# Feed-forward down products: token sums by halves, a second group one piece later, and last blocks between last products

## What is computed

```python
def swiglu(x, w_gate, w_up, w_down):
    return (jax.nn.silu(x @ w_gate) * (x @ w_up)) @ w_down

x = x + 0.5 * swiglu(rmsnorm(x, ffn1_norm[l]), ffn1_w_gate[l], ffn1_w_up[l], ffn1_w_down[l])
```

## Time and profile before

| what | value |
|---|---|
| median of three runs | 1376.59 us |
| the profiled execution | 1378.8 us |
| its span, first to last instruction | 1377.0 us |
| TensorE (PE) busy | 1331.3 us, 97% |
| VectorE (DVE) busy | 930.1 us, 68% |
| ScalarE (ACT) busy | 817.0 us, 59% |
| GpSimd (POOL) busy | 476.5 us, 35% |
| mean granted TensorE clock | 0.987 |

### The profile page before, as it was taken

One profiled execution on the slowest core, in us unless ns is written; L12 is line 12 of the kernel. 1 busy time (PEld: TensorE's weight loads), 2 busy tenths in 40 slices (PEclk: granted clock), 3 DMA queues, 4 the chain that ended last, 5 costly groups with the idle time before them and its releaser, 6 DMA issues.

```text
span 1377.0 us, 18310 instructions
## 1 busy us (share of the span) xinstructions
PE 1331.3 (97%) x7264; PEld 1119.2 (81%) x7264; DVE 930.1 (68%) x1162; ACT 817.0 (59%) x1095; POOL 476.5 (35%) x220
## 2 busy tenths in 40 slices
PE   9999899999999899999799999999999999999988
PEld 8878777888878788878688887788888888887877
DVE  6678876955669796678785659764335642568887
ACT  7654557457656457655457687667434654665553
POOL 1614013464550504432313431134535524452410
PEclk9999999999999999999999999999999999999999
DMA  9586983324659685668784656345755543648783
GB/s 338 184 235 219 248 269 131 115 93 153 209 148 287 167 266 205 204 159 269 175 282 148 225 180 214 118 158 174 286 182 174 178 168 127 224 154 203 233 221 108
DMA packets 42278, 269.66 MB, mean 196 GB/s; under 512 B 6320, under 2 KB 6864, under 8 KB 11216
## 3 DMA queue, kind: packets, MB, share of 16 engines
q1 hardware_dynamic: 35680, 226.69, 46.8%
q0 software_dynamic: 4608, 33.56, 13.3%
q10 hardware_dynamic: 1904, 8.23, 1.7%
HBM read 267.38 MB, written 1.08 MB: 195 GB/s over the span
## 4 chain that ended last, share of the span: by engine, by line
PE 64%; DVE 16%; POOL 9%; ACT 4%; DMA 3%; issue 2%; SPq 1%; POOLq 0%; ACTq 0%; DVEq 0%
PE acc L392 12%; PE acc L394 11%; PE acc L393 11%; PE acc L407 9%; DVE wlo L373 8%; PE acc L408 5%; POOL forms L1027 4%; POOL forms L1019 4%; DMA raw<-in_t_ffn_down 2%; PE acc L2828 2%; DVE x L936 2%; PE work L661 1%; DVE work L864 1%; DVE form_lo L927 1%; PE work L662 1%
## 5 line engine op out<-in xcount | busy, mean ns | idle before, releaser
L373 DVE TENSOR_TENSOR wlo<-raw,whi 128x2048 fp32r<-128x2048 f32 (+1 forms) x189 | 443.6, 2350 | 125.9 <-ACT whi L368 125.7
L368 ACT ACTIVATE whi<-raw 128x2048 fp32r<-128x2048 f32 (+1 forms) x245 | 460.4, 1886 | 61.1 <-PE acc L394 25.0
L407 PE MATMUL acc<-xT,whi 128*128 128x512 f32 x1208 | 429.8, 398 | 1.4 <-DVE wlo L373 1.3
L373 POOL TENSOR_TENSOR wlo<-raw,whi 128x2048 fp32r<-128x2048 f32 x56 | 270.7, 4835 | 374.7 <-ACT whi L368 366.8
L408 PE MATMUL acc<-xT,wlo 128*128 128x256 f32 x1384 | 373.9, 281 | 0.0
L407 PEld LDWEIGHTS acc<-xT,whi 128*128 128x128 f32 x1208 | 227.0, 188 | 56.2 <-issue 2.5
L408 PEld LDWEIGHTS acc<-xT,wlo 128*128 128x128 f32 x1384 | 261.5, 189 | 7.1
L392 PE MATMUL acc<-whi,xT 128*128 128x512 f32 x416 | 168.4, 405 | 0.0
L394 PE MATMUL acc<-whi,xT 128*128 128x512 f32 x416 | 162.5, 391 | 0.0
L393 PE MATMUL acc<-wlo,xT 128*128 128x512 f32 x416 | 162.3, 390 | 0.0
L774 ACT ACTIVATE hid_hi<-work 128x256 fp32r<-128x256 f32 x88 | 33.7, 383 | 134.1 <-DVE work L873 134.1
(11 more groups left out here) (422 smaller groups left out, 2135.3 us busy)
## 6 DMA issues: line engine op xcount, KB each, us to landing
raw<-in_t_ffn_up SPq DMA_DIRECT2D x85, 1024.0 KB, 5.4
raw<-in_t_m_in SPq DMA_DIRECT2D x52, 1024.0 KB, 5.2
raw<-in_t_ffn_down SPq DMA_DIRECT2D x32, 1024.0 KB, 6.2
raw<-in_t_ffn_down POOLq DMA_DIRECT2D x32, 1024.0 KB, 8.6
raw<-in_t_m_os SPq DMA_DIRECT2D x8, 1024.0 KB, 4.9
raw<-in_t_ffn_down SPq DMA_DIRECT2D x8, 512.0 KB, 4.3
raw<-in_t_m_out SPq DMA_DIRECT2D x4, 1024.0 KB, 5.1
sum_rows<-row_scratch ACTq DMA_DIRECT2D x4, 1024.0 KB, 4.7
```

Of the source, the lines that this page charges most:

```text
L368: act.activation(granule(whi, u, i), granule(raw, u, i), ACT.Copy).then_inc(hi_ready, 1)
L373: eng.tensor_tensor(granule(wlo, u, i), granule(raw, u, i), granule(whi, u, i).bitcast(F32), ALU.subtract).then_inc(lo_signal(g)[0], 1)
L407: pe.matmul(to, hi[:, c], both_parts(kt), start=first, stop=False)
```

## The change

Three things move. GpSimd's two token sums of a group are issued one by one (`sum_hidden(group, j)`), each as soon as its four hidden rows are there, and in other places of its queue. In the order of places the second group starts one piece later. And the last four blocks alternate with the last four products of the second group. Waits, `hi` and `lo` follow the new order; the last two places become places like the others, so that by tokens only the last two rows are multiplied in the last stage.

Places 10 to 39 after: 10 to 24 as before, up18 (25), P4' (26), up19, P6' (28), up20, P3' (30), up21, P7' (32), b0 (16 to 19), P1' (34), b0 (20, 21), P2' (36), b1 (16 to 19) (37), P5' (38), b1 (20, 21) (39). The transposes stand behind place 37.

```diff
 def late_places():
-    for k in range(11):
+    for k in range(len(PRODUCTS)):
         places += [products[k], ("up", 11 + k)]
-    blocks = [("block", half, kts) for half in range(2) for kts in ((16, 17, 18, 19), (20, 21))]
-    return places + [products[11], blocks[0], products[12], blocks[1], products[13], blocks[2], blocks[3]]
+    places.append(("up", 18))
+    for k in range(3):
+        places += [products[7 + k], ("up", 19 + k)]
+    for k, (half, kts) in enumerate(((0, (16, 17, 18, 19)), (0, (20, 21)), (1, (16, 17, 18, 19)), (1, (20, 21)))):
+        places += [products[10 + k], ("block", half, kts)]
+    return places
...
 def multiply_by_token(pe, u, xhi, xlo, banks, last_bank):
-            for i in range(2):
-                if t == 0 and i == 1:
-                    wait_lo(pe, u.g + 1)
-                hi, lo = granule(whi, u, i), granule(wlo, u, i)
-                for j, kt in enumerate(u.granules[i]):
-                    mm = triple(pe, to, xhi, xlo, kt, t, hi[:, j, c], lo[:, j, c], i == 0 and j == 0,
-                                i == 1 and j == len(u.granules[1]) - 1)
+            hi, lo = granule(whi, u, 0), granule(wlo, u, 0)
+            for j, kt in enumerate(u.granules[0]):
+                mm = triple(pe, to, xhi, xlo, kt, t, hi[:, j, c], lo[:, j, c], own and j == 0, j == len(u.granules[0]) - 1)
...
 ffn_tensor:
-                if n == LAST_UNIT - 1 and b + 1 != B_OUT:
-                    transpose_x(pe, b + 1, 0)
...
-                if f == 3 and half == 1:
-                    if n == LAST_UNIT:
-                        multiply_by_token(pe, u, hid_hi, hid_lo, BACK_OF_X, ffn_banks(NCH)[0][:, 0:256])
+                if f == 3 and n == PLACES - 1:
+                    multiply_by_token(pe, u, hid_hi, hid_lo, BACK_OF_X, ffn_banks(NCH)[0][:, 0:256])
                 else:
                     multiply(pe, u, i, hid_hi, hid_lo, ffn_banks(NCH + half), kts[0] == 16, kts[-1] == KFF - 1)
+                if n == 37 and b + 1 != B_OUT:
+                    transpose_x(pe, b + 1, 0)
...
 ffn_scalar:
-            if n == 23:
-                act.wait_ge(gran_done, place_done(f, n))
+            if n == 24:
                 round_forms(1)
-        square_x(act, b + 1, 0)
-        if b + 1 == B_FFN2:
-            square_gained(act, 0)
-        hi(LAST_UNIT + 3)
+            if n == 36:
+                square_x(act, b + 1, 0)
+                if b + 1 == B_FFN2:
+                    square_gained(act, 0)
...
 ffn_vector:
-            if n in (10, 24):
-                rest_forms((10, 24).index(n))
+            if n in (10, 25):
+                rest_forms((10, 25).index(n))
+            if n == 35:
+                for t in range(NT):
+                    dve.wait_ge(*last_added[t, 0])
+                residual_half(dve, b + 1, 0, place_done(f, n), ffn_banks(NCH), HALF_RSTD)
+                if b + 1 == B_FFN2:
+                    apply_final1(dve, 0)
...
             elif entry[0] == "product":
-                if n < 35:
+                if n < 38:
                     lo(n + 3)
-                if n == 35:
-                    lo(38)
-                    lo(39)
                 add_product(n, *entry[1:])
-                if n == 37:
-                    if b == B_FFN0:
-                        dve.wait_ge(params_loaded, 16 * len(PARAMS))
-                    if b + 1 != B_OUT:
-                        rest_xt(dve, b + 1, 0)
-            elif n == 34:
+            elif n < 37:
                 lo(n + 3)
-            elif n == 36:
-                for t in range(NT):
-                    dve.wait_ge(*last_added[t, 0])
-                residual_half(dve, b + 1, 0, place_done(f, n), ffn_banks(NCH), HALF_RSTD)
-                if b + 1 == B_FFN2:
-                    apply_final1(dve, 0)
-                lo(PLACES)
+            elif n == 37:
+                lo(n + 3)
+                if b == B_FFN0:
+                    dve.wait_ge(params_loaded, 16 * len(PARAMS))
+                if b + 1 != B_OUT:
+                    rest_xt(dve, b + 1, 0)
...
 ffn_pool:
-        def make_forms(group):
-            pool.wait_ge(hidlo_done, PIECES * f + KD * (group + 1))
+        def sum_hidden(group, j):
+            pool.wait_ge(hidlo_done, PIECES * f + KD * group + 4 * (j + 1))
             if group:
                 pool.wait_ge(forms_split, 2 * (2 * f + 1))
-            for j in range(2):
-                kts, rows = slice(4 * j, 4 * j + 4), slice(KD * group + 4 * j, KD * group + 4 * j + 4)
-                link(pool, pool.tensor_tensor(forms[:, kts, :], hid_hi[:, rows, :].bitcast(F32), hid_lo[:, rows, :].bitcast(F32),
-                                              ALU.add))
+            kts, rows = slice(4 * j, 4 * j + 4), slice(KD * group + 4 * j, KD * group + 4 * j + 4)
+            link(pool, pool.tensor_tensor(forms[:, kts, :], hid_hi[:, rows, :].bitcast(F32), hid_lo[:, rows, :].bitcast(F32),
+                                          ALU.add))
+
+        def make_forms():
             form((1, 1), (1, 0), ALU.subtract)
...
-        lo(9)
         if b == B_FFN2:
             pool.wait_ge(x_rescaled, NT)
-        make_forms(0)
+        sum_hidden(0, 0)
+        split_lo(pool, *place(f, 9))
+        sum_hidden(0, 1)
+        make_forms()
         add_to_slot(15)
         add_to_slot(17)
+        sum_hidden(1, 0)
         add_to_slot(19)
         add_to_slot(23)
-        make_forms(1)
-        add_to_slot(29)
-        add_to_slot(31)
-        add_to_slot(33)
-        add_to_slot(37)
+        sum_hidden(1, 1)
+        make_forms()
+        add_to_slot(30)
+        add_to_slot(32)
+        add_to_slot(34)
+        add_to_slot(38)
```

More of the change, by code:

```diff
@@ L70 @@
            "P5": ((1, 1, 1),)}
-LATE_FROM, PLACES, LAST_UNIT = 10, 40, 38
-UPS_BY_GPSIMD = ()
+LATE_FROM, PLACES = 10, 40
 def late_places():
@@ L78, in late_places @@
     places = [("up", 10)]
-    for k in range(11):
+    for k in range(len(PRODUCTS)):
         places += [products[k], ("up", 11 + k)]
-    blocks = [("block", half, kts) for half in range(2) for kts in ((16, 17, 18, 19), (20, 21))]
-    return places + [products[11], blocks[0], products[12], blocks[1], products[13], blocks[2], blocks[3]]
+    places.append(("up", 18))
[4 more added lines that the diff above has]
+    return places
 LATE = dict(enumerate(late_places(), LATE_FROM))
+PLACE_OF_PIECE = {entry[1]: n for n, entry in LATE.items() if entry[0] == "up"}
 def rows_of(entry):
@@ L118, in add_ffn @@
             add(f"ffn{f}.up{c}", [tuple(range(KD))] * 2)
-        for n in range(LATE_FROM, LAST_UNIT):
+        for n in range(LATE_FROM, PLACES):
             add(f"ffn{f}.place{n}", [rows_of(LATE[n])])
-        add(f"ffn{f}.last", [rows_of(LATE[n]) for n in range(LAST_UNIT, PLACES)])
     add_ffn(0)
@@ L171, in build @@
     first_of = [units[f"ffn{f}.up0"].g for f in range(4)]
-    late_split_by_vector = {first_of[f] + n: entry[0] != "up" or entry[1] % 2 == 0 or entry[1] not in UPS_BY_GPSIMD
-                            for f in range(4) for n, entry in LATE.items()}
+    split_in_late_place = {first_of[f] + n for f in range(4) for n in LATE}
     added = {first_of[f] + n for f in range(4) for n, entry in LATE.items()
@@ L282, in build @@
     products_added = sem("products_added")
-    added_to_slot = {slot: sem(f"added_to_slot{slot}") for slot in (1, 3)}
+    added_to_slot = {slot: sem(f"added_to_slot{slot}") for slot in range(RING)}
     final_rows_loaded = sem("final_rows_loaded")
@@ L297, in lo_signal @@
     def lo_signal(g):
-        by_vector = [n for n in range(g + 1) if late_split_by_vector.get(n, n % 2 == 0)]
+        by_vector = [n for n in range(g + 1) if n % 2 == 0 or n in split_in_late_place]
         if g in by_vector:
@@ L584, in place @@
             return units[f"ffn{f}.up{n // 2}"], n % 2
-        if n < LAST_UNIT:
-            return units[f"ffn{f}.place{n}"], 0
-        return units[f"ffn{f}.last"], n - LAST_UNIT
+        return units[f"ffn{f}.place{n}"], 0
     def place_done(f, n):
@@ L592, in place_of_piece @@
     def place_of_piece(m):
-        return m if m <= LATE_FROM else LATE_FROM + 2 * (m - LATE_FROM)
+        return PLACE_OF_PIECE.get(m, m)
     def ffn_loads(sp, f):
@@ L833, in ffn_scalar @@
         hi(8)
-        for n in range(5, LAST_UNIT):
+        for n in range(5, 38):
             entry = LATE.get(n, ("up", n))
@@ L840, in ffn_scalar @@
                 round_hidden(entry[1])
-            elif n < LAST_UNIT - 1:
+            else:
                 hi(n + 4)
@@ L955, in lo @@
                     split_lo(dve, next_units[0], 0)
-            elif n < LATE_FROM and n % 2 == 0 or n >= LATE_FROM and late_split_by_vector[first_of[f] + n]:
+            elif n % 2 == 0 or n >= LATE_FROM:
                 split_lo(dve, *place(f, n))
@@ L960, in ffn_vector @@
             entry = LATE.get(n, ("up", n))
-            if n in (10, 24):
-                rest_forms((10, 24).index(n))
+            if n in (10, 25):
+                rest_forms((10, 25).index(n))
```

(26 more changed lines are left out.)

4 lines of the change are left out of this document (removed).

## The result

The changed kernel takes **1360.89 us** (median of 4 runs, 1358.47 to 1361.13), the kernel before, run beside it, 1377.09 (4 runs, 1376.2 to 1377.63). The ratio is 0.9879, with a 95% interval of 0.9862 to 0.9896: 16.2 us or 1.2% faster. The forecast was 1365, in an own range of 1357 to 1371. The profiled execution took 1361.1 us, its span is 1359.3, 17.7 less than before, and TensorE's mean granted clock 0.991 for 0.987.

A forecast was written before the change was run, and what follows sets the result against it. The prediction took TensorE's own waits in the four feed-forward stages, 53 us of excess, as the bound. Its terms left 41.5, 11.5 us less, so 1376.6 became 1365 us; own range 1357 to 1371, with rivals 1342 to 1376.

The forecast's parts named there:

- What bounds the kernel: TensorE's own waits in the late places of feed-forward stages F0 to F3: 53 us of excess, the most to gain.
- Step 1: First group's P6 in the four stages: its 2.14 us idle goes, excess falls from 14 to 2.6 us.
- Step 2: First group's P1: add_to_slot(19) goes out 6 us late behind a GpSimd sum; new stalls, 16.1 us in all.
- Step 3: Second group's P6: TensorE waits about 1.5 us and 0.6 behind it; 8.4 us in all, for 30 before.
- step 6: Clock behind the new stalls: four drops to half clock at 1.6 us each, 6.4 us.
- Step 4: Stage ends: waits before transposes go; 0.5, 2 and 0.5 us stay, plus 2 for F0's parameter loads.
- Step 5: Tail of F3: the last residual starts some 3.1 us behind the last matmul, +3 us.
- forecast case: P1 stalls 2.8 us with the median landing, whole kernel 1365 us; chance 0.50.
- Rival A: Add of place 19 comes in time, no P1 stall: 1344 us, or 1334 without second P6 stall; chance 0.30.
- Rival B: All four adds of place 19 land in 12.0 us, P1 stalls 6.2 each, every clock drop: 1383; chance 0.12.
- Rival C: Second group's P6 still stands 4 us and loses its clock in each stage: 1380 or 1375 us; chance 0.08.

The follow-up runs named there:

- e5: The kernel before, order of places kept, with token sums by halves and the second group's first sum behind add_to_slot(19): 1358.15 us, ratio 0.9865.
- e7: The changed kernel with its new order alone: both sums of a group wait for the whole group, in their old queue places: 1355.49 us, ratio 0.9846.
- e8: The changed kernel with sum_hidden(1, 0) behind add_to_slot(19) and sum_hidden(0, 0) behind GpSimd's split of place 9: 1336.22 us, ratio 0.9704.
- e1: The changed kernel with one line moved, the second group's first sum behind add_to_slot(19) instead of ahead of it: 1336.94 us, ratio 0.9706.
- e2: The changed kernel with the second group's first sum made twice in a row ahead of add_to_slot(19): 1377.05 us, ratio 0.9999.
- e6: As e1, with both blocks of F3's last half multiplied token half by token half behind P5': 1337.18 us, ratio 0.9708.
- e4: The changed kernel with each group's sums together, behind the split of place 9 and add_to_slot(23), each keeping its own wait: 1347.04 us, ratio 0.978.
- e3: The kernel before, order of places kept, with token sums by halves and the second group's first sum ahead of add_to_slot(19): 1379.68 us, ratio 1.002.

## Why the prediction was right, step by step

**What bounds the kernel** held: TensorE's own waits. Every run's span follows from the sum of its excess to a little over 1 us (e5: 53 less 33.8 is 19.2, the span fell by 18.3; e7: 24.1 and 24.2).

**Step 1** was right: 2.6 forecast, 2.5 measured. The reason given for a part of it, the first sum put ahead of the split of place 9, was not needed (e8); it is that the first sum no longer stands behind hid_lo of piece 7, and that GpSimd's last sum then runs in 2.40 us.

**Step 2** carried the forecast, and e1 and e2 show it. In the times of before I had the sum's end at 421.1, the add at 421.7, the landing at 430.3, the split's end at 435.9 and P1 due at 433.2; the trace has 420.9, 421.2, 430.8, 436.6 and 433.4. The landing took 9.6 us, 1.0 more than the median that I had taken, and the add went out 0.5 us sooner, so two errors cancel in part. The sum's own terms: 13.3 for the idles, 14.7 measured; 2.8 for what stands behind, of which nothing was seen apart from the clock.

**Step 3** was right in its mechanism and too large: 8.4 forecast, 5.0 measured. VectorE's chain was right to 0.3 us (the split for the second P6 starts at 469.67 and ends at 471.95, in the times of after; I had 471.66). It was TensorE that came later than I put it, since I priced the half clock behind P1 in step 6 and did not carry its 1.6 us on to the time at which TensorE reaches the second P6. Two stalls in a row aren't independent: the first takes from the second. Of the 5.0 only 3.2 are the second P6's own, as said above.

**Step 4** was mis-sized: 5 forecast, 2.3 measured. F0's ends show 0.9 in all. The 2 us set aside for its parameter loads may stand elsewhere, in the 1.5 us of P3' that the account books under the second P6; with these the step is 3.8 for 5. F1 shows 1.4, of which 0.54 is an idle for `xT`.

**Step 5** was right: 3 forecast, 3.3 measured, and e6 gives it back where its stated cause is undone.

**Step 6** was near in size by an error each way: all four P1 products lost the clock, where I took three, for 7.3 us, and no second P6 did, where I took one. That the two errors nearly cancel is luck.

**The sum** was 6.4 us too high: 3.4 from step 3, 2.7 from step 4, 1.4 from step 2, less 0.9 and 0.3 from steps 6 and 5, and 0.1 from step 1. The time is only 4.1 us below the forecast, since the profiled executions lie further apart than the medians. The forecast case happened, with its stall at P1; 1360.9 lies in its own range.

**Rival A** (the add in time, 1344, or 1334 with no stall of the second P6) did not occur, but e1 makes its case by another way and measures 1336.9. Its price was near. Neither of its conditions arose: the landing of 5.8 us was far off (8.3 was the least of 32), and the engines were within 1 us of my times at place 19. The fit of the Trainium skill, "DMA: Bandwidth & Descriptors", section "Anatomy of one DMA", from which I estimated 4.4 us for 1 MB, does not agree with these adding transfers either, which took 8.3 to 11.7 us. **Rival B** (1383) did not occur in full: the four landings at place 19 were 9.3 to 10.2 us, where it had 12.0; of its clock drops P1's fourth came, and none of P6's. **Rival C** is wrong: no second P6 waits more than 0.6 us.

## What to carry to other kernels

In a queue that runs in order, an early-issued piece of work belongs behind the instruction that starts a transfer, not ahead of it: moving 4.4 us of slack work past one DMA issue was worth 24 us here, more than half of the 39.8 that the change gives with it. When two stalls stand in one chain, carry the first one's delay, its clock loss too, into the due time of the second. And judge an edit by the account of places, not by the time alone: in e6 a gain of 3.3 us and a new wait of 2.8 us looked like no effect.

## What the runs showed of the hardware

**Who pays for VectorE and GpSimd side by side.** The one that starts later pays nearly the whole of the other's time: a GpSimd sum of 2.40 us took 4.39 when a split had just started (changed kernel, e1), and a split of 2.28 took 4.71 when a sum had started 0.19 us before it (e4). I had expected the sum to wait, and not that 0.2 us would decide which engine does. The Trainium skill, "SBUF — State Buffer", section "SBUF: two separate sides", states that rule: of a GpSimd instruction that reads SBUF and a VectorE instruction with two SBUF inputs, whichever starts first has the shared ports for its whole instruction, and the other blocks. The sums and the splits are of these kinds, and the rows agree: a sum 0.17 us behind a split waits 2.0 us, a split 0.19 us behind a sum 2.4.

**The clock does not follow from the length of the idle alone.** In the kernel before, an idle of 2.14 us was followed by the full clock in F1, and one of 2.13 us at the same place in F0 (the product from 80.55 on) by half clock for most of the product; in e7 the idles of 2.13 to 2.15 us were all followed by the full clock. The longer ones up to 4 us were followed by either level. In e5 the windows behind the four idles of 3.18, 3.28, 2.92 and 2.82 us read:

```profile
140.80:145.20 4.40, 4.32 (x12) 3.45 (x13) 3.95 (x5) 3.89 (x4) 0.86 (x1) 0.61 0.61 97
467.60:471.00 3.40, 2.98 (x12) 2.17 (x12) 2.95 (x4) 2.90 (x4) 0.87 (x1) 1.00 0.50 58
657.70:662.90 5.20, 5.13 (x12) 4.09 (x13) 4.75 (x6) 4.58 (x4) 0.86 (x1) 0.50 0.66 110
1300.90:1305.10 4.20, 4.20 (x12) 3.33 (x13) 3.75 (x5) 3.82 (x4) 0.87 (x1) 0.64 0.58 96
```

The longest of the four kept the full clock (1.00), the others fell to 1.2 GHz for the product or most of it. In e3 the P1 idles of 3.14 and 3.18 us cost no clock, in the changed kernel one of 3.18 cost all of the product. All idles of 7.3 us and more in e2 were followed by half clock. What else decides, these runs do not show.
